# HGRN keys carried as logarithms, zero products ahead of the first transposes, and both compressions in one slab

## The reference

```python
f = lb + (1.0 - lb) * jax.nn.sigmoid(f_logits)       # HGRN2: forget value, its key is 1 - f
logf, k = jnp.log(f), 1.0 - f
A = jnp.cumsum(lf, axis=2)
rel = jnp.where(tri, A[:, :, :, None, :] - A[:, :, None, :, :], -jnp.inf)
att = jnp.einsum('bhtd,bhsd,bhtsd->bhts', qq, kk, jnp.exp(rel))
...
o_c = rms_norm(o_c, hgrn_norm[l].reshape(HG_HEADS, HG_VDIM))

ck = jnp.einsum('bcpgd,pde->bcge', kc[:, cidx] + pe_k[:, None, :], w_ck)   # compressed keys
cv = jnp.einsum('bcpgd,pde->bcge', vc[:, cidx] + pe_v[:, None, :], w_cv)   # compressed values
```

## Time and profile before

| | |
|---|---|
| median of three runs | 491.39 us |
| the profiled execution | 491.25 us, span 489.4 us |
| PE busy | 474.8 us, 97% |
| DVE, ACT, POOL busy | 359.8, 255.9, 157.4 us |
| granted PE clock | 0.999, mean of the span |
| DVE clears PM | from 0.87, 0.27 us |
| DMA | 76.43 MB, mean 156 GB/s |
| chain that ended last | PE 88%, DVE 9% |

### The profile page before, as it was taken

One profiled execution on the slowest core, in us unless ns is written; L12 is line 12 of the kernel. 1 busy time (PEld: TensorE's weight loads), 2 busy tenths in 40 slices (PEclk: granted clock), 3 DMA queues, 4 the chain that ended last, 5 costly groups with the idle time before them and its releaser, 6 DMA issues.

```text
span 489.4 us, 9629 instructions
## 1 busy us (share of the span) xinstructions
PE 474.8 (97%) x3938; PEld 462.8 (95%) x3938; DVE 359.8 (74%) x647; ACT 255.9 (52%) x379; POOL 157.4 (32%) x157
## 2 busy tenths in 40 slices
PE   3999999999999999999999999999999999999995
PEld 3999999999899999999999999999999999999995
DVE  4897999899978775989696755888674357655653
ACT  6966635363484555844366444566554245433541
POOL 1072800702800006992067334546645220000000
PEclk9999999999999999999999999999999999999999
DMA  9965553325525485355537235234435535767502
GB/s 298 322 193 176 173 173 93 98 86 173 173 88 172 137 209 173 97 173 174 171 107 239 87 90 168 88 102 158 130 129 173 174 95 192 232 218 255 173 1 86
DMA packets 77030, 76.43 MB, mean 156 GB/s; under 512 B 6783, under 2 KB 75775, under 8 KB 76987
## 3 DMA queue, kind: packets, MB, share of 16 engines
q1 hardware_dynamic: 76699, 75.64, 49.5%
q10 hardware_dynamic: 288, 0.18, 0.2%
HBM read 74.77 MB, written 1.05 MB: 155 GB/s over the span
## 4 chain that ended last, share of the span: by engine, by line
PE 88%; DVE 9%; DMA 1%; issue 1%; ACT 0%; DVEq 0%
PE ps L970 71%; PE ps L1142 3%; DVE WL L603 3%; PE ps L995 2%; PE ps L1094 2%; PE ps L1083 1%; PE ps L1158 1%; DVE R L648 1%; DVE CP L813 1%; DVE R L649 1%; PE ps L1110 1%; DMA R<-x 1%; DVE PM L716 1%; PE ps L1097 1%; PE ps L1112 1%
## 5 line engine op out<-in xcount | busy, mean ns | idle before, releaser
L970 PE MATMUL ps<-hH,WL 128*128 128x256 f32 x696 | 200.6, 288 | 1.0 <-DVE WL L603 1.0
L970 PE MATMUL ps<-hL,WH 128*128 128x256 f32 x696 | 197.7, 284 | 0.0
L970 PE MATMUL ps<-hH,WH 128*128 128x256 f32 x696 | 197.7, 284 | 0.0
L603 DVE TENSOR_TENSOR WL<-W,WH 128x2048 fp32r<-128x2048 f32 x66 | 152.2, 2307 | 16.1 <-PE ps L970 15.7
L420 ACT ACTIVATE WH<-W 128x2048 fp32r<-128x2048 f32 x66 | 124.6, 1889 | 58.4 <-PE ps L970 58.3
L970 PEld LDWEIGHTS ps<-hH,WL 128*128 128x128 f32 x696 | 132.8, 191 | 2.2 <-DVE WL L603 1.2
L970 PEld LDWEIGHTS ps<-hL,WH 128*128 128x128 f32 x696 | 132.8, 191 | 0.8 <-issue 0.7
L970 PEld LDWEIGHTS ps<-hH,WH 128*128 128x128 f32 x696 | 132.8, 191 | 0.0
L381 POOL TENSOR_SCALAR R<-R,st 128x256 f32<-128x256 f32 x32 | 29.2, 923 | 80.1 <-DVE st L782 80.1
L970 PE MATMUL ps<-bH,WL 128*128 128x256 f32 x192 | 54.9, 286 | 0.0
L970 PE MATMUL ps<-bL,WH 128*128 128x256 f32 x192 | 54.3, 283 | 0.0
(11 more groups left out here) (191 smaller groups left out, 756.0 us busy)
## 6 DMA issues: line engine op xcount, KB each, us to landing
W<-w_in SPq DMA_DIRECT2D x49, 1024.0 KB, 5.2
W<-w_branch SPq DMA_DIRECT2D x12, 1024.0 KB, 5.0
W<-w_out SPq DMA_DIRECT2D x4, 1024.0 KB, 5.4
R<-x SPq DMA_DIRECT2D x2, 512.0 KB, 4.6
W<-w_in SPq DMA_DIRECT2D x2, 512.0 KB, 6.7
R<-cmp_w SPq DMA_DIRECT2D x2, 512.0 KB, 8.4
OC<-pool_w SPq DMA_DIRECT2D x4, 256.0 KB, 5.8
R<-x SPq DMA_DIRECT2D x1, 1024.0 KB, 7.2
```

Source lines behind the costliest of these rows:

```text
L603: dve.tensor_tensor(WL[:, s % 2, :, 0:n], W[:, s % 3, :, 0:n], WH[:, s % 3, :, 0:n], ALU.subtract).then_inc(s_lo, 1)
L970: mm = pe.matmul(o, l, r, start=(k == 0 and j == 0 and not (split and c)), stop=(k == KC - 1 and j == 2 and not (split and not c)))
```

## The change

It has five parts. (1) PE multiplies zeros 18 times ahead of the transposes; the zeros are a part of PM that DVE clears first. (2) `first_product` mixes its three kinds of steps, and slab 1 runs its 32 matmuls with WH ahead of the 16 with WL, waiting for WL only there. (3) HK becomes f - 1, at most -1e-30; ACT takes ln(-HK) next to ln f; DVE subtracts HA from it behind the scan; POOL adds block edges to that, so that the exponential already holds the key, and DVE multiplies by the query alone. The first level's key half is one exponential a head with a bias. (4) The normalisation (L639) moves one slab on, to 15, 19, 23 and 27. (5) Keys and values are compressed together at s = 27, alternating between the upper and the lower 64 columns of the array.

```diff
@@ gpsimd, for each pair p @@
+                k2 = HK[:, 2 * p:2 * p + 2, :].rearrange("p h t -> p (h t)")
                 for i, b in enumerate(LEVELS):
+                    if i == 0:
+                        continue
...
-                    last = pool.tensor_tensor(dv[:, :, 0:b], edge, av[:, :, 0:b], ALU.subtract)
-                    if i:
-                        pool.tensor_tensor(dv[:, :, b:2 * b], av[:, :, b:2 * b], edge, ALU.subtract)
+                    pool.tensor_tensor(dv[:, :, 0:b], kv[:, :, 0:b], edge, ALU.add)
+                    pool.tensor_tensor(dv[:, :, b:2 * b], av[:, :, b:2 * b], edge, ALU.subtract)
...
+                                   k2.rearrange("p (n w) -> p n w", w=4), mid, ALU.add)
+                pool.tensor_tensor(QK[p % 2][:, SMALL_Q].rearrange("p h (n w) -> p (h n) w", w=4),
                                    a2.rearrange("p (n w) -> p n w", w=4), mid, ALU.subtract).then_inc(s_sub, 1)
@@ scalar @@
+                        act.activation(k, k, ACT.Ln, scale=-1.0)
                         act.activation(f, f, ACT.Ln).then_inc(s_ln, 1)
...
-                        act.activation(q[:, 0, :, 0:P], q[:, 0, :, 0:P], ACT.Exp)
-                        act.activation(q[:, 1:NLV].rearrange("p l h t -> p (l h t)"),
-                                       q[:, 1:NLV].rearrange("p l h t -> p (l h t)"), ACT.Exp)
-                        small = q[:, SMALL_K].rearrange("p h t -> p (h t)")
-                        act.activation(q[:, SMALL_Q].rearrange("p h t -> p (h t)"), small, ACT.Exp)
-                        act.activation(small, small, ACT.Exp, scale=-1.0).then_inc(s_hexp, 1)
+                        for e in range(2):
+                            act.activation(q[:, 0, e, 0:P], HK[:, 2 * p + e, 0:P], ACT.Exp,
+                                           bias=HA[:, 2 * p + e, P - 1:P])
+                        act.activation(q[:, 1:].rearrange("p l h t -> p (l h t)"),
+                                       q[:, 1:].rearrange("p l h t -> p (l h t)"), ACT.Exp).then_inc(s_hexp, 1)
...
-                    act.wait_ge(s_cpe, 1)
+                    act.wait_ge(s_cpe, 2)
@@ vector @@
-                link(dve.tensor_scalar(HK[:, 2 * p:2 * p + 2, :], OC[:, 2 * p:2 * p + 2, :], -1.0, 1.0,
-                                       ALU.mult, ALU.add))
+                link(dve.tensor_scalar(HK[:, 2 * p:2 * p + 2, :], OC[:, 2 * p:2 * p + 2, :], 1.0, -1e-30,
+                                       ALU.subtract, ALU.min))
...
                     link(last)
+                    dve.tensor_tensor(HK[:, 2 * p:2 * p + 2], HK[:, 2 * p:2 * p + 2], HA[:, 2 * p:2 * p + 2], ALU.subtract)
...
-                    if s == U0 + 5 + 4 * (h // 2):
+                    if s == U0 + 6 + 4 * (h // 2):
                         dve.wait_ge(s_hrs, h // 2 + 1)
...
-                            dve.tensor_tensor(ev[:, :, 0:b], ev[:, :, 0:b], kv[:, :, 0:b], ALU.mult)
                             dve.tensor_tensor(ev[:, :, b:2 * b], ev[:, :, b:2 * b], qv[:, :, b:2 * b], ALU.mult)
-                        dve.tensor_tensor(sk, sk, HK[:, h], ALU.mult)
                         dve.tensor_tensor(sq_, sq_, HQ[:, h], ALU.mult).then_inc(s_hmul, 1)
...
+            dve.memset(PM[:, :, 0:P], 0.0).then_inc(s_zero, 1)
             dve.memset(st_eps, EPS).then_inc(s_init, 1)
-            dve.memset(PM[:, :, 0:P], 0.0)
@@ tensor @@
-                pe.wait_ge(s_lo, s + 1)
+                if s == 1:
+                    pe.wait_ge(s_hi, 1)
+                else:
+                    pe.wait_ge(s_lo, s + 1)
...
+                if s == 1:
+                    order.sort(key=lambda ckj: ckj[2] == 0)
+                for at, (c, k, j) in enumerate(order):
+                    if s == 1 and at == 4 * KC:
+                        pe.wait_ge(s_lo, s + 1)
...
-                mm.then_inc(s_cpe, 1)
+                    keys, values = (cpe[:, a, j].rearrange("p g c -> p (g c)") for a in range(2))
+                    end = dict(start=(j == 0), stop=(j == CB // 2 - 1))
+                    mk = pe.matmul(ck_out.rearrange("p g c -> p (g c)"), WC[:, 0, j, :], keys, **end)
+                    mv = pe.matmul(ps[0:GROUPS * NCMP, 6, 0:HEAD], values, WC[:, 1, j, :], **end)
...
-                steps = [(WH, hH, k) for k in range(KC)] + [(WH, hL, k) for k in range(KC)] \
-                    + [(WL, hH, k) for k in range(KC)]
+                high, low, rest = ([(w, h, k) for k in range(KC)] for w, h in ((WH, hH), (WH, hL), (WL, hH)))
+                steps = high[0:2] + rest[0:2] + [high[2], rest[2], high[3], rest[3], low[0]]
+                for k in range(4, KC):
+                    steps += [high[k], low[k - 3]]
+                steps += low[KC - 3:] + rest[4:]
...
+            pe.wait_ge(s_zero, 1)
+            for _ in range(WARM):
+                pe.matmul(ps[:, 7, 0:P], PM[:, 0, 0:P], PM[:, 1, 0:P], start=True, stop=True)
```

More of the change, by code:

```diff
@@ L86 @@
 NU = HG * TT
+WARM = 18
 def trunk(nc, x, small, consts, w_in, cmp_w, pool_w, w_branch, w_out, post_norm, out):
@@ L525, in read @@
                     else:
-                        act.wait_ge(s_hmul, 4 * (n - 1))
+                        act.wait_ge(s_sub, 2 * (n - 1))
+                        act.wait_ge(s_hexp, 2 * (n - 1))
                     for src, own, other in query_halves(s):
@@ L949, in product @@
                 split = kind == "out" and n == 0
-                order = [(c, k) for c in range(1 if kind == "gate" else 2) for k in range(KC)]
+                order = [(c, k, j) for c in range(1 if kind == "gate" else 2) for k in range(KC) for j in range(3)]
+                mixed = split or s == 1
                 if split:
-                    order.sort(key=lambda ck: ck[1])
-                for c, k in order:
+                    order.sort(key=lambda ckj: ckj[1])
+                if s == 1:
[3 more added lines that the diff above has]
+                        pe.wait_ge(s_lo, s + 1)
                     if kind == "branch" and n == 0 and c == 0 and k % 2 == 0:
@@ L959, in product @@
                         o = last_rows(c) if s == NS - 1 else bank(s)[:, w * c:w * c + w]
-                        pairs = [(a[:, k, P * c:P * c + P], b[:, k, 0:w])
-                                 for a, b in ((ah, wl), (al, wh), (ah, wh))]
+                        a, b = ((ah, wl), (al, wh), (ah, wh))[j]
+                        l, r = a[:, k, P * c:P * c + P], b[:, k, 0:w]
                     else:
@@ L966, in product @@
                             o = bank(s)[0:GATES, 0:T]
-                        pairs = [(b[:, k, P * c:P * c + m], a[:, k, :])
-                                 for a, b in ((ah, wl), (al, wh), (ah, wh))]
-                    for j, (l, r) in enumerate(pairs):
-                        mm = pe.matmul(o, l, r, start=(k == 0 and j == 0 and not (split and c)),
-                                       stop=(k == KC - 1 and j == 2 and not (split and not c)))
-                        if small:
-                            i, h = small.pop(0)
-                            last = compressed_scores(i, h)
-                            if not small:
-                                last.then_inc(s_cpe, 1)
-                    if s == NS - 1 and k == KC - 1:
+                        a, b = ((ah, wl), (al, wh), (ah, wh))[j]
+                        l, r = b[:, k, P * c:P * c + m], a[:, k, :]
+                    mm = pe.matmul(o, l, r, start=(at == 0 if mixed else k == 0 and j == 0),
+                                   stop=(at == len(order) - 1 if mixed else k == KC - 1 and j == 2))
+                    if small:
+                        i, h = small.pop(0)
+                        last = compressed_scores(i, h)
+                        if not small:
+                            last.then_inc(s_cpe, 1)
+                    if s == NS - 1 and k == KC - 1 and j == 2:
                         mm.then_inc(s_last, 1)
@@ L1014, in hg_values, with compress @@
                 mm.then_inc(s_hpv, 1)
-            def compress(a):
+            def compress():
                 pe.wait_ge(s_cw, 32)
                 pe.wait_ge(s_read_v, DVE_READS[WHERE[("vc", 0)]])
-                if a:
-                    pe.wait_ge(s_hoc, HG)
+                pe.wait_ge(s_hoc, HG)
                 for j in range(CB // 2):
-                    rows = cpe[:, a, j].rearrange("p g c -> p (g c)")
-                    if a:
-                        mm = pe.matmul(ps[0:GROUPS * NCMP, 6, 0:HEAD], rows, WC[:, a, j, :],
-                                       start=(j == 0), stop=(j == CB // 2 - 1))
-                    else:
-                        mm = pe.matmul(ps[0:HEAD, 5, 0:GROUPS * NCMP], WC[:, a, j, :], rows,
-                                       start=(j == 0), stop=(j == CB // 2 - 1))
-                mm.then_inc(s_cpe, 1)
+                    keys, values = (cpe[:, a, j].rearrange("p g c -> p (g c)") for a in range(2))
+                    end = dict(start=(j == 0), stop=(j == CB // 2 - 1))
```

(12 more changed lines are left out.)

14 lines of the change are left out of this document (7 added, 7 removed).

## The result

The changed kernel takes 487.41 us (median of four runs, 487.32 to 488.93) against 491.41 in the same runs: a ratio of 0.9926, 95% interval 0.9909 to 0.9943. The forecast was 486.9 in a range of 485.0 to 488.7. The profiled execution took 487.49 us with a span of 485.7, 3.7 less than before. DVE is busy 352.1 us (359.8 before), PE 477.4 (474.8: the zeros are in it), POOL 160.0, ACT 258.1.

The account below looks back on a forecast made before the run. PE was taken to bound the kernel, being busy nearly the whole span. Start -1.65, DVE's relief -2.4 and compression with moved normalisation -0.4 sum to -4.45 us, giving 486.9 us in a range of 485.0 to 488.7.

Parts of the forecast that it names:

- The clock at the start: Start: zeros raise PE's clock before the transposes; with the new step order slab 1 starts at 15.5, not 17.17: -1.65 us.
- The bound of the start: Start: if the zeros help nothing, the two reorderings alone still let PE pack, slab 1 at 16.4: -0.75 us.
- Slabs 2 to 8: DVE's low part of slab 4 ends near 32.0, 0.8 us ahead of PE: narrow, but no wait.
- The relief of DVE: Halved multiplications remove PE's waits on WL at slabs 9 and 15, leaving 0.2 at 17: -2.4 us.
- The one visit: Slab 27: compressing keys and values together takes PE 2.6 us, with the array's halves partly beside each other.
- Slab 29: The moved normalisation delays ACT's gate and DVE's copy; PE waits about 0.9 us, leaving -0.4 us with the merged compression.
- the 1.35 us that PE wins: PE reaches slab 29 1.35 us earlier through the merged compression, between 0 and 1.9.
- A: Rival, chance 0.17: no new wait at slab 29, array halves wholly beside each other; -6.2 us, 485.1.
- B: Rival, chance 0.18: the zeros do not help and part of the slab 17 wait stays; -2.85 us, 488.4.
- C: Rival, chance 0.07: DVE and POOL hinder each other in slabs 2 to 7; +3.2 us, 494.4.

Follow-up runs that it names:

- e1: The changed kernel without the 18 zero products ahead of the transposes; 488.20 us (0.9934).
- e12: The kernel of e10 with 9 zero products instead of 18; 486.49 us (0.9898).
- e10: e7 plus the copy of the compressed values moved to slab 27, ahead of the key split's gate and slab 29's low part; 485.16 us (0.9870).
- e11: The kernel of e10 with 14 zero products instead of 18; 485.39 us (0.9876).
- e7: The changed kernel with DVE's low part of slab 28 made ahead of its reads of slab 26; 485.89 us (0.9888).
- e13: The changed kernel with four small products of ones on PE inside each wait, ahead of slabs 28 and 29; 487.32 us (0.9916).
- e8: The kernel before the change with the logarithmic keys alone; 488.79 us (0.9946).
- e3: The changed kernel with the normalisation put back by a slab, to 14, 18, 22 and 26; 486.35 us (0.9898).
- e4: The changed kernel with values compressed in slab 28 again, keys in slab 27, normalisation in its new place; 487.16 us (0.9916).
- e5: The changed kernel with the last pair's normalisation back in slab 26 and DVE's low part 28 ahead of its slab 26 reads; 487.02 us (0.9909).

## Why the prediction was right, and where its steps failed

- **The clock at the start.** Right that zeros bring the clock up ahead of the transposes. Mis-sized: the zeros' records kept the slow spacing (0.21 us) until 6.7, 5.5 us from their start and not 3.3, so that they lasted until 7.9 and not 7.0. The transposes began at 7.94, half a microsecond late, and hH at 9.30 instead of 8.9. The term was -1.65 and measured -1.37.
- **The bound of the start.** "The two reorderings alone, -0.75" did not come out in the execution of e1 that was traced: slab 1 starts at 17.07, since the first high steps also ran at the slow spacing, to 11.9. In the kernel before the slow spacing ended at 10.2 and in e12 at 10.4, so that one late rise of the clock can be chance; the other executions were not traced. Yet e1's median is only 0.8 us behind the change, for of the 1.27 at slab 1 it has 0.99 left at the last step of slab 8 (63.03 against 62.04): the earlier start is partly waited off.
- **Slabs 2 to 8.** The narrow place was there, but at slab 6 rather than 4, and the slack was overdrawn: 0.2 to 0.4 us of small gaps on WL at slab 6 after, in e10 and in e11, and in e11 ahead of slab 3 too. In e7 and e13 the zeros took 5.7 and 5.6 us and slab 1 began at 15.47 and 15.39, as early as forecast, and nothing came of it: wherever slab 1 began between 15.4 and 15.95, the last step of slab 8 came at 61.7 to 62.1.
- **The relief of DVE.** Right in place and near in size: -2.4 forecast, -2.45 between slabs 1 and 17, -2.5 by e8. The waits at 9, 15 and 17 are nil. I had left 0.2 at slab 17, which is gone too, and slabs 2 to 8 took as much, so that the agreement to 0.05 is luck.
- **The one visit.** 64 records take 2.00 us (195.20 to 197.20), not 2.6: the key records and the value records each keep the spacing of 0.06 us that a compression had alone, so the two halves of the array work wholly beside each other. The Trainium skill ("TensorEngine Tiling (Array Packing)", Key Properties) says that different tiles can load weights and multiply in parallel, and these rows agree. The rule in the Trainium skill ("TensorE: Matmul & The Clock Gate", Part 3, The mechanism) that a weight load overlaps a running product only in another row group does not hold in them: the prediction put it at near 3.4 us.
- **Slab 29.** Right in its path: ACT's gate stands behind the normalisation and PE waits for the copy, and e3 shows the cause. Mis-sized: the copy came 1.80 us later against DVE's reads of slab 26, the upper end of the forecast's 1.1 to 1.8, where the sum took the middle. The last pair's normalisation took 1.91 us where 0.9 to 1.65 was allowed, and the second half of the gate (L843) 1.28 for 0.77; a faster low part of slab 29 (2.28 for 3.12) gave some of it back. Since the copy had been ready only 1.9 us ahead of PE, the term came out at 0 where -0.4 was forecast. That the wait itself measured 0.96 against 0.9 is luck: PE came some 0.3 later than forecast, because the visit gave 0.6 more and slab 28 took 0.9, and the copy came 0.4 later too.
- **Slab 28.** A step that the prediction left out. It carried the 1.35 us that PE wins straight to slab 29. Between them lies slab 28, whose low part had been covered by the second compression. Its wait of 0.87 made nothing later here, as e4 shows, but it is a second bound that counts as soon as the copy is early: e3, without the wait for the copy, keeps 0.90 at slab 28 and takes 13.88 us from slab 27 to slab 29, where e10, without either wait, takes 12.73.
- **The rivals.** A had the halves of the array right and the missing wait wrong. B fell with the transposes at 0.12. Of C only the gap at slab 6 came true: POOL is busy 2.6 us longer in all, a good way from the blocks of 17 us that it needed.

The terms now read -1.37 - 2.45 + 0 = -3.8, against -3.7 of span and -4.0 of median. The forecast's -4.45 was 0.6 too much, half of it in the start and most of the rest at slab 29.

## What to carry to other kernels

Work that is taken off the bounding engine uncovers every wait that it had hidden, not only the one that is watched: go through each step between the saving and the place where it is to be cashed, and ask of each operand how long it has been ready. When such a wait appears, look for what stands ahead of the late instruction in its engine's queue and isn't needed yet; two moved operations turned 487.4 into 485.2 here, and a third move, made for the same reason, lost 1.1 (e5 against e7). And where an engine waits twice in a row, follow the chain back from the last wait: the first may cost nothing until the last is gone.

## What the runs showed of the hardware

- The clock of PE rises while it multiplies zeros: the changed kernel's records of them begin 0.21 us apart until 6.7 and 0.11 apart from there, and the transposes behind them 0.11; behind e12's 18 records, all 0.21 apart, and 2.08 us of waiting the transposes begin 0.21 apart again. In the kernel before, the spacing falls from 0.21 to 0.11 at 10.2, within the transposes. The granted clock is printed as 1.00 throughout, and only the spacing of equal records tells the level at the start. How long the 36 take differs from one execution to the next (5.6 to 7.1 us), and slab 1 with it.
- Two waits of about 0.9 us, 7 us apart, were followed in 7 of 26 executions by a loss of 1.3 to 2.0 us, more than either wait; in the two of them that were traced, about 3.4 us ran at the granted clock of 0.50. That the waits are the cause is supported by where it appears and not proved.
- Products on the two column halves of the array, with their own weights, run beside each other in full: 32 pairs at 0.06 us a pair.
